# Two feed-forward up products with x as the still operand, 512 weight columns moving, and the gated block turned on TensorE

## The chip, the cores and the metric

One NeuronCore of one Trainium2 chip runs the whole program. The metric is the device time of one execution in microseconds (us). Everything is float32 at the interface; the products run as sums of three matmuls on operands that are split into a high and a low part, so one mathematical matmul is three on TensorE (PE).

## The reference, cut to what matters

Two transformer-like blocks follow one another on 256 tokens (T) by 2048 channels (D). They hold three feed-forward layers with 5632 hidden channels. The first one has a convolution over the tokens between its up product and its gate; the second and the third, which are what is changed here, do not:

```
def _swiglu(x, wg, wu, wd):
    return (jax.nn.silu(x @ wg) * (x @ wu)) @ wd

h = x
f1 = _swiglu(_rmsnorm(h, ffn1_pre_g[l]), ffn1_w_gate[l], ffn1_w_up[l], ffn1_w_down[l])
h = h + 0.5 * _rmsnorm(f1, ffn1_post_g[l])
...
f2 = _swiglu(_rmsnorm(h, ffn2_pre_g[l]), ffn2_w_gate[l], ffn2_w_up[l], ffn2_w_down[l])
h = h + 0.5 * _rmsnorm(f2, ffn2_post_g[l])
```

`wg` and `wu` are 2048 x 5632, `wd` is 5632 x 2048. The norm's factor of a token (one over the root of its mean square, called rs below) is a number per token, and so it can be multiplied in behind the product.

## The kernel before

**Units.** All large weights stream through four slots of `stage`, 1 MB each (128 partitions x 2048 float32 columns). One slot's content is a *unit*. SyncE (SP) issues one DMA per unit as soon as the unit four places ahead has been split. ScalarE (ACT, line 792) writes the high part of the slot into one of two `w_hi` buffers, VectorE (DVE, line 1303) writes the rest into `w_lo`, and PE multiplies. Semaphore `split_made` tells PE that a unit is split, `split_used` tells ACT that PE is done with the unit two before, so that its buffer can be written again. A unit is 12288 moving columns on PE wherever it is used in a feed-forward layer.

**One feed-forward layer** (`ffn(n)`, n is 0, 1 or 2; n = 1 and 2 are "the second and third") has two parts of 24 and 20 chunks of 128 hidden channels (`PARTS`). A part has an up stage, two units per chunk (88 per layer, 176 in the second and third together), and a down stage, one unit per chunk.

- *Up, before* (`wide_steps`, lines 2264 to 2268): the unit is all 2048 rows of 128 columns of gate or up. For each of its 16 row chunks the weights stand still and x moves: a matmul with `w_hi` still and 512 columns moving (the high and the low part of x side by side, line 2267), then one with `w_lo` still and 256 columns moving (line 2268). The last row chunk has the two in the other order (2264, 2265). That is 32 matmuls per unit. The results have hidden channels on the partitions and tokens along the row. Units alternate gate, up, gate, up; two of them are a *pair*. ACT copies half of a pair's sums out of PSUM (line 877), DVE adds the other half (1499), multiplies by rs (1509, from `rsb`, rs laid along the row by a small matmul in `rs_rows`, line 2422), ACT applies silu (892), DVE multiplies gate by up (1532), ACT writes `hid_hi` (897) and DVE `hid_lo` (1314). These stand between the splits in a fixed order (`up_body_order`, line 665). Most pairs run in hardware loops (`Fori`).
- *Down* (`rows_half`, line 2304): the chunk of `hid_hi` or `hid_lo` stands still and 512 weight columns move, 24 matmuls per unit (2335, 2336, 2339; in the last unit of a layer 2322 to 2324, which reports its two column quarters one after the other). The products with x itself as the still operand (`in_rows`, `out1`, `out2`) use the same lines with `xt`.

**Entering a layer.** x is turned on PE (`norm(n)`, line 2384, 128x128 transposes in groups of four: two row chunks of two token tiles), scaled into `xt` by ACT (857) and DVE (1354). `norm_done` counts the groups that are ready, eight in all. Before the third layer all 32 transposes stand ahead of the first up matmul, and for the second layer groups 0 to 3 are turned early, in the down stage ahead (`turn_early`), and groups 4 to 7 between pieces of the first two units. Those first two units are run side by side (`first_two`, `tile_part`), each piece waiting for its groups. Units 2 and 3 follow.

**Between the units of the second layer** PE also builds tables for a position bias (`bias_rows`, line 2431), after three pairs of units per side; POOL loads its inputs when DVE has written `x_nat` (`x_made`) and copies its results out, paced by `split_used`.

The engines' programs are written out by hand; each engine works in the order of its own code.

Of the kernel before, what the change touches and what calls it, by code (L numbers as in the profile page):

```python
# [24 lines left out]
F32 = mybir.dt.float32  # L25
# [13 lines left out]
PARTS = ((0, 24), (24, 20))  # L39
EPS = 1e-6  # L40
# [59 lines left out]
def build(nc, I, out):  # L100
# [10 lines left out]
    def sb(name, cols, dt=F32, at=None, parts=P):  # L111
# [32 lines left out]
    rsb = sb("rsb", T, at=TT + 6144)  # L144
# [124 lines left out]
        quarter diag_made rsb_made small_in pos_made pos_copied raw_made hn_gelu ht_made ht_copied kv_made  # L269
# [65 lines left out]
    def _(sp):  # L335
# [49 lines left out]

        def load_ffn(n):
            f = ffn_w[n]
            for part, (f0, chunks) in enumerate(PARTS):
                load(f"up{n}{part}", 4, chunks // 2, pairs(f["up"], f["off"], f0))
# [265 lines left out]
    def turn_bank(n, g):  # L655

        if n == 2:
            return (0, 1, 2, 3, 2, 3, 4, 6)[g]
        return 4 + g % 4 if n else g

    PAIR_BANK = (0, 4)

# [119 lines left out]
    def _(act):  # L782
# [35 lines left out]
        def square_pieces(e, src, p, first=0, step=2):  # L818

            for m in range(MT):  # L820
                act.wait_ge(S["piece_made"], PIECE_AT[e] + step * p + m + 1 + first // 3)
                square(src[:, span(p, m)], first + 3 * m + p, SSQ_AT[e] + step * p + m + first // 3)
# [38 lines left out]
        def ffn(n, boundary, after):  # L861
            conv = ffn_w[n]["conv"]
            for part, (f0, chunks) in enumerate(PARTS):
# [6 lines left out]
                def e0(j, s):  # L870

                    act.wait_ge(split_used, 2 * j + (before + 4))
                    if conv:
                        act.wait_ge(S["pair_d1"], j + (q0 + 1))
                    else:
                        act.wait_ge(S["pair_d2"], j + (q0 - 1))
# [12 lines left out]
                def e2(j, s):  # L889
                    act.wait_ge(S["pair_d1"], j + (q0 + 3))  # L890
                    src = conv_a[:, s * T:(s + 1) * T] if conv else turn[:, s * 512:s * 512 + T]
                    act.activation(conv_a[:, s * T:(s + 1) * T], src, ACT.Silu).then_inc(S["pair_e2"], 1)
# [7 lines left out]
                up_phase(act, lambda i, u: split(name, 4, i, u), e2, e3, e1 if conv else nothing, chunks, split_down,  # L900
                         boundary=None if part else boundary, s0=e0)
                for u in range(2, chunks):
                    split_down(u)
                    if part:
# [138 lines left out]
        def enter_ffn1(split):  # L1043

            split(0)
            split(1)
            square_pieces(2, x_nat, 1, 0, 4)
            scaled_hi(2, 4, C_F1)
            scaled_hi(2, 5, C_F1)
            square_pieces(2, f_nat, 1, 6, 4)  # L1050
            square_pieces(2, x_nat, 2, 0, 4)
            scaled_hi(2, 6, C_F1)
            scaled_hi(2, 7, C_F1)
            square_pieces(2, f_nat, 2, 6, 4)
            root(2, 4)
# [15 lines left out]
        def enter_ffn2(split):  # L1071
# [4 lines left out]
            for g in range(4):  # L1076
                scaled_hi(4, g, C_F2)
            act.wait_ge(S["piece_made"], NEW_AT[6] + 4)
            for m in range(MT):
                square(x_nat[:, m * D:m * D + HALF], 2 * m, SSQ_AT[7] + m)  # L1080
            for g in range(4, 8):
# [1941 lines left out]
```

## Time and profile before

| | |
|---|---|
| median of 3 runs | 3593.45 us (3589.94 to 3593.74) |
| the profiled execution | 3594.03 us, span 3592.1 us |
| PE matmul busy | 3425.2 us, 95% |
| DVE busy | 2130.7 us, 59% |
| ACT busy | 1636.2 us, 46% |
| DMA | mean 198 GB/s |

The span runs from the first to the last instruction, and 1.9 us of the execution lie around it. Matmul durations in the rows run from a matmul's start to its modelled end, and matmuls overlap; the pace of PE is read from start to start.

### The profile page before, as it was taken

Reading aid. Unit: us, or ns where it says so; the run is one execution under the profiler, and the core shown is the slowest. Engines: PE = TensorE matmul, PEld = TensorE weight load, DVE = VectorE, ACT = ScalarE, POOL = GpSimd, SP = SyncE. Lnnn points to the kernel's source line nnn. Section 1 sums busy time; section 2 is a strip of 40 time slices with the busy share of each in tenths; the row PEclk is TensorE's granted clock in tenths of the full one; section 3 lists DMA queues with packets and bytes.
Section 4 is the critical chain, followed back from the end, with each engine's and each line's share of the span. In section 5 each row is a group of like instructions: output and inputs, shape, how many; then the busy total and the mean of one; then the engine's idle time right before and its main releaser. Section 6 shows DMA issues by size and latency. Waiting matters only on the chain.

```text
span 3592.1 us, 49777 instructions
## 1 busy us (share of the span) xinstructions
PE 3425.2 (95%) x19694; PEld 2919.4 (81%) x19694; DVE 2130.7 (59%) x2280; ACT 1636.2 (46%) x1772; POOL 346.2 (10%) x411
## 2 busy tenths in 40 slices
PE   5899889999999999999999899999999899999998
PEld 1786678888888888888888799898888788888886
DVE  0774657775566565544555578895455555545555
ACT  0333346653455455543443455663443555434443
POOL 1110000000000000000000147661000000000000
PEclk7899999999999999999999999999899999999999
DMA  9998657776666667976665656667235566666664
GB/s 398 297 340 299 221 167 225 225 227 221 188 187 195 189 186 164 204 206 189 187 187 188 175 149 156 168 179 232 91 106 187 153 187 186 187 189 188 185 188 139
DMA packets 813373, 712.54 MB, mean 198 GB/s; under 512 B 13127, under 2 KB 742527, under 8 KB 805696
## 3 DMA queue, kind: packets, MB, share of 16 engines
q1 hardware_dynamic: 787840, 627.09, 58.9%
q0 software_dynamic: 20624, 79.44, 7.8%
q10 hardware_dynamic: 4784, 4.27, 0.4%
q8 instruction: 88, 1.44, 0.2%
q14 instruction: 37, 0.30, 0.0%
HBM read 698.94 MB, written 11.80 MB: 198 GB/s over the span
## 4 chain that ended last, share of the span: by engine, by line
PE 78%; DVE 9%; ACT 4%; DMA 4%; issue 3%; POOL 1%; ACTq 0%; DVEq 0%; SPq 0%; POOLq 0%
PE ps L2267 24%; PE ps L2268 12%; PE ps L2335 8%; PE ps L2336 8%; PE ps L2339 8%; DVE w_lo L1303 3%; ACT w_hi L792 3%; DMA stage<-in_w_ada 2%; PE ps L2286 2%; PE ps L2287 2%; PE ps L2288 2%; PE ps L2265 2%; PE ps L2299 1%; PE ps L2495 1%; PE ps L2300 1%
## 5 line engine op out<-in xcount | busy, mean ns | idle before, releaser
L1303 DVE TENSOR_TENSOR w_lo<-stage,w_hi 128x2048 fp32r<-128x2048 f32 x528 | 1221.4, 2313 | 1093.7 <-ACT w_hi L792 1092.6
L792 ACT ACTIVATE w_hi<-stage 128x2048 fp32r<-128x2048 f32 x528 | 1010.8, 1914 | 1483.5 <-PE ps L2265 617.0
L2267 PE MATMUL ps<-xt,w_hi 128*128 128x512 f32 x3960 | 1416.2, 400 | 11.3 <-DVE w_lo L1303 10.1
L2268 PE MATMUL ps<-xt,w_lo 128*128 128x256 f32 x3960 | 1114.1, 281 | 0.0
L2267 PEld LDWEIGHTS ps<-xt,w_hi 128*128 128x128 f32 x3960 | 746.9, 189 | 187.8 <-DVE w_lo L1303 14.5
L2268 PEld LDWEIGHTS ps<-xt,w_lo 128*128 128x128 f32 x3960 | 750.9, 190 | 11.8
L2335 PE MATMUL ps<-w_hi,hid_hi 128*128 128x512 f32 x1152 | 449.2, 390 | 5.8 <-DVE w_lo L1303 5.8
L2336 PE MATMUL ps<-w_lo,hid_hi 128*128 128x512 f32 x1152 | 448.2, 389 | 0.0
L2286 PE MATMUL ps<-xt,w_hi 128*128 128x256 f32 x1184 | 342.2, 289 | 18.9 <-DVE w_lo L1303 16.6
L2339 PE MATMUL ps<-w_hi,hid_lo 128*128 128x512 f32 x1152 | 354.7, 389 | 0.0
L2287 PE MATMUL ps<-xt,w_hi 128*128 128x256 f32 x1184 | 337.0, 285 | 0.0
L2288 PE MATMUL ps<-xt,w_lo 128*128 128x256 f32 x1184 | 336.8, 284 | 0.0
L2335 PEld LDWEIGHTS ps<-w_hi,hid_hi 128*128 128x128 f32 x1152 | 216.2, 188 | 52.4 <-DVE w_lo L1303 4.3
L2286 PEld LDWEIGHTS ps<-xt,w_hi 128*128 128x128 f32 x1184 | 229.0, 193 | 29.8 <-issue 23.6
L2339 PEld LDWEIGHTS ps<-w_hi,hid_lo 128*128 128x128 f32 x1152 | 216.2, 188 | 45.0
L2336 PEld LDWEIGHTS ps<-w_lo,hid_hi 128*128 128x128 f32 x1152 | 216.3, 188 | 44.7
L2287 PEld LDWEIGHTS ps<-xt,w_hi 128*128 128x128 f32 x1184 | 229.3, 194 | 0.0
L2288 PEld LDWEIGHTS ps<-xt,w_lo 128*128 128x128 f32 x1184 | 229.1, 193 | 0.0
L2335 PE MATMUL ps<-w_hi,xt 128*128 128x512 f32 x248 | 98.4, 397 | 8.7 <-issue 3.2
L2265 PE MATMUL ps<-xt,w_hi 128*128 128x512 f32 x264 | 105.4, 399 | 0.0
L2495 PE MATMUL ps<-stage,csilu 128*32 128x512 f32 x384 | 68.3, 808 | 33.6 <-DMA stage<-in_w_ada 33.1
L2336 PE MATMUL ps<-w_lo,xt 128*128 128x512 f32 x248 | 97.2, 392 | 0.0
(414 smaller groups left out, 3649.9 us busy)
## 6 DMA issues: line engine op xcount, KB each, us to landing
stage<-in_w_in SPq DMA_DIRECT2D x92, 1024.0 KB, 5.7
stage<-in_w_up SPq DMA_DIRECT2D x88, 1024.0 KB, 5.8
stage<-in_ffn_w_gate SPq DMA_DIRECT2D x88, 1024.0 KB, 5.6
stage<-in_ffn_w_up SPq DMA_DIRECT2D x88, 1024.0 KB, 5.6
stage<-in_ffn_w_down SPq DMA_DIRECT2D x88, 1024.0 KB, 5.5
stage<-in_w_ada SPq DMA_DIRECT2D x48, 1024.0 KB, 8.8
stage<-in_w_down SPq DMA_DIRECT2D x44, 1024.0 KB, 5.1
late<-in_w_ada POOLq DMA_DIRECT2D x64, 512.0 KB, 6.7
```

The source lines that it names most:

```text
L792: act.activation(w_hi[:, u % 2 * UNIT:(u % 2 + 1) * UNIT], slot(u % SLOTS), ACT.Copy).then_inc(hi_made, 1)
L1303: dve.tensor_tensor(w_lo[:, part], slot(u % SLOTS), w_hi[:, part].bitcast(F32), ALU.subtract).then_inc(split_made, 1)
L2265: last = pe.matmul(dst, wh, both(k), start=False, stop=True)
L2267: pe.matmul(dst, wh, both(k), start=k == 0, stop=False)
L2268: last = pe.matmul(dst[:, T:2 * T], wl, chunk(xt_hi, k), start=False, stop=False)
L2286: pe.matmul(dst, wh, chunk(xh, k0 + k), start=start and k == 0, stop=False)
L2287: pe.matmul(dst, wh, chunk(xl, k0 + k), start=False, stop=False)
L2288: last = pe.matmul(dst, wl, chunk(xh, k0 + k), start=False, stop=stop and k == n - 1)
L2335: pe.matmul(rows_cols(half, m, n, 512, swapped), a, wh, start=st, stop=False)
L2336: pe.matmul(rows_cols(half, m, n, 512, swapped), a, wl, start=False, stop=False)
L2339: last = pe.matmul(rows_cols(half, m, n, 512, swapped), b, wh, start=False, stop=en)
L2495: last = pe.matmul(ps[32 * j:32 * j + 32, b * 512:(b + 1) * 512], weight.to_broadcast([P, 32]), part[:, j % 2 * 512:(j % 2 + 1) * 512], st ...
```

## The change

In the second and third layer (`ffn_rows(n)` on ACT, DVE and PE takes the place of `ffn(n)`), the hidden channels go by *blocks* of four chunks: six blocks in the first part, five in the second, 22 in the two layers.

- A unit of the up stage is now 512 rows (four row chunks) of 512 weight columns of gate or up. A block has 8 units: gate and up by turns for each of four groups of rows. SP loads it so (`blocks_of`), with runs of 512 columns per row where there were 128.
- On PE a row chunk of x for one token tile stands still and 512 weight columns move: x high by `w_hi`, x high by `w_lo`, x low by `w_hi`, 24 matmuls per unit. The sums of a block stand in four banks with tokens on the partitions (gate: two, up: two), blocks alternate between the two halves of PSUM.
- rs is now a number per partition: ACT reads the gate's bank, scales by rs and applies silu in one instruction (`gate`, two per block), DVE multiplies up's bank by rs and by that (`product`, two per block, into `h_blk`). PE turns `h_blk` by eight 128x128 transposes (`turn_hid`) after the second unit of the next block, back into the gate's two banks; ACT and DVE make `hid_hi` and `hid_lo` from there (`hidden`, two instructions each). `rs_rows`, `take_rs` and `rsb` are gone.
- No hardware loop is left in these two layers.
- The entry: only groups 0 and 1 of x must be ready for units 0 and 1, two more groups for each further pair of units. The transposes of the rest stand behind unit 0, 1 (and 2 for the third layer), four row chunks each. ACT's and DVE's splits, squares and scalings are put in a matching order.
- `bias_rows` stands behind unit 11, as before behind 12 units, and uses other banks. Which half of the down product takes which banks is exchanged between the parts.

The core of the diff:

```diff
+        def blocks_of(ws, f0):
+            views = [w.rearrange("(c k p) n -> c p k n", p=P, k=4) for w in ws]
+            return lambda i, u: [(slot(u % SLOTS).rearrange("p (k n) -> p k n", k=4),
+                                  views[u % 2][u // 2][:, :, ds(i * 512 + f0 * P, 512)])]
...
+                def unit(v):
+                    j, u = divmod(v, 8)
+                    pe.wait_ge(split_made, plan[up][1] + v + 1)
+                    for kk in range(4):
+                        k, at = 4 * (u // 2) + kk, v % 2 * UNIT + kk * 512
+                        wh, wl = (w[:, at:at + 512] for w in (w_hi, w_lo))
+                        for m in range(MT):
+                            dst = bank(block_bank(j, u % 2, m))
+                            pe.matmul(dst, chunk(xt_hi, k, m), wh, start=k == 0, stop=False)
+                            pe.matmul(dst, chunk(xt_hi, k, m), wl, start=False, stop=False)
+                            last = pe.matmul(dst, chunk(xt_lo, k, m), wh, start=False, stop=k == KC - 1)
+                    last.then_inc(split_used, 1)
...
+                def turn_hid(j):
+                    pe.wait_ge(S["pair_d2"], block_at(n, part, j) + 1)
+                    for c in range(4):
+                        for m in range(MT):
+                            last = pe.transpose(bank(block_bank(j, 0, c // 2), c % 2 * T + m * P, P),
+                                                h_blk[:, m * 512 + c * P:m * 512 + (c + 1) * P], ident[:, :])
+                    last.then_inc(S["hid_turned"], 1)
...
+                    unit(v)
+                    if part == 0 and j == 0:
+                        between(u)
+                    if j and u == 1:
+                        turn_hid(j - 1)
+                    if n == 1 and part == 0 and v == 11:
+                        bias_rows()
...
-        norm(4)
-        ffn(2)
+        norm(4, range(2))
+        def norm_ffn2(u):
+            if u < 3:
+                norm(4, range(2 + 2 * u, 4 + 2 * u))
+        ffn_rows(2, norm_ffn2)
```

ACT and DVE, per block j (v counts the units of the part, u those of the block; DVE's `product` stands at u == 1, all `hidden` at u == 3):

```diff
+                def gate(j):
+                    act.wait_ge(S["norm_rs"], ROOT_AT[RS_ROOT[n]] + 1)
+                    act.wait_ge(split_used, plan[up][1] + 8 * j + 9)
+                    for m in range(MT):
+                        at = RS_COL[n] + m
+                        last = act.activation(turn[:, m * 512:(m + 1) * 512], bank(block_bank(j, 0, m)), ACT.Silu,
+                                              scale=stats[:, at:at + 1])
+                    last.then_inc(S["pair_e2"], 1)
...
+                def product(j):
+                    dve.wait_ge(S["pair_e2"], block_at(n, part, j) + 1)
+                    dve.wait_ge(split_used, plan[up][1] + 8 * j + 10)
+                    for m in range(MT):
+                        last = dve.scalar_tensor_tensor(out=h_blk[:, m * 512:(m + 1) * 512],
+                                                        in0=bank(block_bank(j, 1, m)), scalar=stats[:, at:at + 1],
+                                                        in1=turn[:, m * 512:(m + 1) * 512], op0=ALU.mult, op1=ALU.mult)
+                    last.then_inc(S["pair_d2"], 1)
```

**Where the order moves, first place.** PE at the entry of the third layer, behind the last down matmuls of the product ahead (`out2`; `ident` marks a transpose). Before:

```order
L2323 MATMUL ps<-w_lo,hid_hi 128x512
L2324 MATMUL ps<-w_hi,hid_lo 128x512
L2384 MATMUL ps<-ident,x_nat 128x128 x32
L2267 MATMUL ps<-xt,w_hi 128x512
L2268 MATMUL ps<-xt,w_lo 128x256
```

And now:

```order
L2432 MATMUL ps<-w_hi,hid_lo 128x512
L2492 MATMUL ps<-ident,x_nat 128x128 x8
L2585 MATMUL ps<-w_hi,xt 128x512
L2586 MATMUL ps<-w_lo,xt 128x512
L2587 MATMUL ps<-w_hi,xt 128x512
...
L2492 MATMUL ps<-ident,x_nat 128x128 x8
L2585 MATMUL ps<-w_hi,xt 128x512
```

Eight transposes are ahead of the first up matmul instead of 32; the other 24 stand in eights behind units 0, 1 and 2.

**Second place.** DVE at the same entry (L1445 and L1509 write the new x, L1354 and L1423 its scaled low part, L1303 and L1372 split a unit). Before:

```order
L1445 SCALAR_TENSOR_TENSOR x_nat<-f_nat,stats,x_nat 128x512 x4
L1354 SCALAR_TENSOR_TENSOR xt<-ps,cols,xt 128x256 x4
L1303 TENSOR_TENSOR w_lo<-stage,w_hi 128x2048
L1445 SCALAR_TENSOR_TENSOR x_nat<-f_nat,stats,x_nat 128x512 x2
L1354 SCALAR_TENSOR_TENSOR xt<-ps,cols,xt 128x256 x4
L1445 SCALAR_TENSOR_TENSOR x_nat<-f_nat,stats,x_nat 128x512 x2
L1354 SCALAR_TENSOR_TENSOR xt<-ps,cols,xt 128x256 x8
L1319 TENSOR_REDUCE stats<-stats 128x2
L1323 TENSOR_SCALAR stats<-stats 128x2
L1303 TENSOR_TENSOR w_lo<-stage,w_hi 128x2048
```

And now:

```order
L1509 SCALAR_TENSOR_TENSOR x_nat<-f_nat,stats,x_nat 128x512 x2
L1423 SCALAR_TENSOR_TENSOR xt<-ps,cols,xt 128x256 x4
L1372 TENSOR_TENSOR w_lo<-stage,w_hi 128x2048
L1509 SCALAR_TENSOR_TENSOR x_nat<-f_nat,stats,x_nat 128x512 x4
L1423 SCALAR_TENSOR_TENSOR xt<-ps,cols,xt 128x256 x4
L1372 TENSOR_TENSOR w_lo<-stage,w_hi 128x2048
L1509 SCALAR_TENSOR_TENSOR x_nat<-f_nat,stats,x_nat 128x512 x2
L1423 SCALAR_TENSOR_TENSOR xt<-ps,cols,xt 128x256 x4
L1372 TENSOR_TENSOR w_lo<-stage,w_hi 128x2048
L1423 SCALAR_TENSOR_TENSOR xt<-ps,cols,xt 128x256 x4
L1372 TENSOR_TENSOR w_lo<-stage,w_hi 128x2048 x2
```

The splits of units 1, 2 and 3 now stand behind two groups of x each, where the split of unit 2 stood behind all eight; the sums for rs come behind the split of unit 5.

**Third place.** DVE in the steady up stage, one block (L1635 is `product`, L1646 `hidden`):

```order
L1372 TENSOR_TENSOR w_lo<-stage,w_hi 128x2048 x6
L1635 SCALAR_TENSOR_TENSOR h_blk<-ps,stats,turn 128x512 x2
L1372 TENSOR_TENSOR w_lo<-stage,w_hi 128x2048 x2
L1646 TENSOR_TENSOR hid_lo<-ps,hid_hi 128x512 x2
L1372 TENSOR_TENSOR w_lo<-stage,w_hi 128x2048 x6
```

Four instructions beside eight splits stand where 16 stood (1499, 1509, 1532 and 1314 for each of four pairs).

## Rows read from the trace of the kernel before

**Rows 1.** Cores: span and mean granted TensorE clock.

```profile
core 0: 3592.1 us, clock 0.970
```

**Rows 2.** Page, part 1: busy us (share), instructions.

```profile
PE 3425.2 (95%) x19694; PEld 2919.4 (81%) x19694; DVE 2130.7 (59%) x2280; ACT 1636.2 (46%) x1772; POOL 346.2 (10%) x411
```

**Rows 3.** Page, part 4: chain that ended last, by engine.

```profile
PE 78%; DVE 9%; ACT 4%; DMA 4%; issue 3%; POOL 1%; ACTq 0%; DVEq 0%; SPq 0%; POOLq 0%
```

**Rows 4.** Page, part 5, costliest group of PE: busy us, mean ns, idle before.

```profile
L2267 PE MATMUL ps<-xt,w_hi 128*128 128x512 f32 x3960 | 1416.2, 400 | 11.3 <-DVE w_lo L1303 10.1
```

**Rows 5.** Timeline, ACT, second layer's up stage: start us, us, form [idle before <-releaser].

```profile
1689.93 1.92 ACT L792 ACTIVATE w_hi<-stage 128x2048 fp32r<-128x2048 f32 x1 [3.73 <-PE ps L2265]
...
1708.65 0.58 ACT L877 ACTIVATE turn<-ps 128x512 f32<-128x512 f32 x1
...
1785.97 1.92 ACT L792 ACTIVATE w_hi<-stage 128x2048 fp32r<-128x2048 f32 x1 [3.44 <-PE ps L2265]
```

**Rows 6.** Timeline, ACT, the product out2 (x-shaped operand still).

```profile
2763.94 1.92 ACT L792 ACTIVATE w_hi<-stage 128x2048 fp32r<-128x2048 f32 x1 [3.52 <-PE ps L2339]
...
2785.70 1.92 ACT L792 ACTIVATE w_hi<-stage 128x2048 fp32r<-128x2048 f32 x1 [3.52 <-PE ps L2339]
```

**Rows 7.** Timeline, PE, last down unit of the first layer and the matmul behind it.

```profile
1254.69 0.39 PE L2322 MATMUL ps<-w_hi,hid_hi 128*128 128x512 f32 x1
...
1260.13 0.39 PE L2267 MATMUL ps<-xt,w_hi 128*128 128x512 f32 x1
```

**Rows 8.** Timeline, PE and ACT, around the early transposes of the first layer's down stage.

```profile
1242.84 0.60 PE L2384 MATMUL ps<-ident,f_nat 128*128 128x128 f32 x4
...
1243.10 1.91 ACT L792 ACTIVATE w_hi<-stage 128x2048 fp32r<-128x2048 f32 x1 [2.88 <-PE ps L2339]
...
1249.02 1.92 ACT L792 ACTIVATE w_hi<-stage 128x2048 fp32r<-128x2048 f32 x1 [3.27 <-PE ps L2339]
```

**Rows 9.** Windows: us, then PE, PEld, DVE, ACT, POOL busy, PEclk, DMA share, GB/s.

```profile
1233.00:1255.00 22.00, 22.00 (x104) 18.17 (x104) 12.41 (x12) 12.44 (x19) 0.00 (x0) 1.00 0.60 173
1260.00:1303.00 43.00, 38.56 (x218) 32.27 (x217) 31.26 (x42) 25.48 (x39) 7.61 (x13) 1.00 0.70 192
2824.00:2837.00 13.00, 7.00 (x33) 6.42 (x34) 11.97 (x21) 7.75 (x18) 0.00 (x0) 0.63 0.53 163
2837.00:2851.00 14.00, 13.19 (x65) 11.16 (x64) 3.62 (x7) 6.05 (x10) 0.00 (x0) 0.85 0.00 1
```

**Rows 10.** Timeline, DVE, entry of the third layer.

```profile
2826.88 1.66 DVE L1354 SCALAR_TENSOR_TENSOR xt<-ps,cols,xt 128x256 fp32r<-128x256 f32 x4 [0.70 <-ACT xt L857]
2828.46 2.28 DVE L1303 TENSOR_TENSOR w_lo<-stage,w_hi 128x2048 fp32r<-128x2048 f32 x1
2830.66 1.41 DVE L1445 SCALAR_TENSOR_TENSOR x_nat<-f_nat,stats,x_nat 128x512 f32<-128x512 f32 x2
...
2854.44 0.68 DVE L1499 TENSOR_TENSOR turn<-turn,ps 128x512 f32<-128x512 f32 x1
```

**Rows 11.** Timeline, PE, entry of the third layer.

```profile
2824.79 3.29 PE L2384 MATMUL ps<-ident,x_nat 128*128 128x128 f32 x16 [6.55 <-DVE x_nat L1445]
...
2836.82 0.78 PE L2267 MATMUL ps<-xt,w_hi 128*128 128x512 f32 x1
...
2851.78 0.50 PE L2267 MATMUL ps<-xt,w_hi 128*128 128x512 f32 x1 [1.60 <-DVE w_lo L1303]
```

**Rows 12.** Timeline, ACT, entry of the third layer: splits of units 2, 5 and 6.

```profile
2847.49 1.92 ACT L792 ACTIVATE w_hi<-stage 128x2048 fp32r<-128x2048 f32 x1 [6.60 <-PE ps L2265]
...
2863.72 1.92 ACT L792 ACTIVATE w_hi<-stage 128x2048 fp32r<-128x2048 f32 x1 [2.33 <-PE ps L2265]
...
2869.28 1.92 ACT L792 ACTIVATE w_hi<-stage 128x2048 fp32r<-128x2048 f32 x1 [2.85 <-PE ps L2265]
```

**Rows 13.** Timeline, PE and ACT, entry of the second layer.

```profile
1278.32 0.50 PE L2267 MATMUL ps<-xt,w_hi 128*128 128x512 f32 x1 [1.79 <-DVE w_lo L1303]
...
1296.62 1.92 ACT L792 ACTIVATE w_hi<-stage 128x2048 fp32r<-128x2048 f32 x1 [3.65 <-PE ps L2265]
```

More of the change, by code:

```diff
@@ L39 @@
 PARTS = ((0, 24), (24, 20))
+BLOCKS = tuple(chunks // 4 for _, chunks in PARTS)
 EPS = 1e-6
@@ L903, in ffn, with ffn_rows, hidden @@
                     split_down(u)
+                    if part:
+                        after(u)
+        def ffn_rows(n, enter, after):
+            for part, (f0, chunks) in enumerate(PARTS):
+                up, down = f"up{n}{part}", f"down{n}{part}"
+                def gate(j):
[6 more added lines that the diff above has]
+                    last.then_inc(S["pair_e2"], 1)
+                def hidden(j):
+                    act.wait_ge(S["hid_turned"], block_at(n, part, j) - FC + 1)
+                    for b in range(2):
+                        at = (4 * j + 2 * b) * T
+                        act.activation(hid_hi[:, at:at + 512], bank(block_bank(j, 0, b)), ACT.Copy).then_inc(S["pair_e3"], 1)
+                for v in range(8 * BLOCKS[part]):
+                    if part or v > 4:
+                        split(up, 0, 0, v)
+                    elif v == 0:
+                        enter(lambda u: split(up, 0, 0, u))
+                    j, u = divmod(v, 8)
+                    if part == 0 and v == 5:
+                        root(RS_ROOT[n], 4 if n == 1 else 2)
+                    if j and u == 0:
+                        gate(j - 1)
+                    elif j and u == 3:
+                        hidden(j - 1)
+                for u in range(chunks):
+                    split(down, 0, 0, u)
+                    if u == 0:
+                        gate(BLOCKS[part] - 1)
+                    elif u == 3:
+                        hidden(BLOCKS[part] - 1)
                     if part:
@@ L1286, in _ @@
                 keep_root_table()
-        ffn(2, enter_ffn2, after_post(8))
+        ffn_rows(2, enter_ffn2, after_post(8))
         post_root(8)
@@ L1363, in spread_rs @@
             last.then_inc(S["diag_made"], 1)
-        def take_rs(count):
-            dve.wait_ge(S["rsb_made"], count)
-            link.then(dve.tensor_copy(rsb[:, :], bank(7, 0, T)))
         def quarter_done(e, p, name):
@@ L1489, in ffn @@
                 pb = PAIR_BANK[part]
-                gating = n == 0 and part == 0
+                gating = part == 0
                 def split_down(u):
@@ L2471, in ffn @@
                     first_pairs()
-                if n == 1 and part == 0:
-                    pairs(1, 3)
-                    bias_rows()
-                    pairs(3, chunks // 2)
-                else:
-                    pairs(part == 0, chunks // 2)
-                if n == 0 and part:
+                pairs(part == 0, chunks // 2)
+                if part:
                     pe.wait_ge(S["mod_made"], 6)
                 rows_phase(f"down{n}{part}", chunks // 2, hid_hi, hid_lo, part == 0, q0 + 2, last=part == 1,
-                           after=turn_early if n == 0 and part else nothing)
+                           after=turn_early if part else nothing)
```

309 lines of the change are left out of this document (183 added, 126 removed).

## The prediction

> **What bounds the kernel now.** I read the cores view first: one core, granted clock 0.970 [rows 1], so PE runs at full clock nearly everywhere. Then the page: PE is busy 95% of the span, DVE 59%, ACT 46% [rows 2], and 78% of the chain that ended last is PE's own work [rows 3]. The largest group is the wider of the up product's two matmul forms [rows 4]; its idle time before is 11.3 us over all layers, so PE is not waiting there, it is working. What matters is therefore PE's pace per unit, and a matmul's printed duration doesn't give it, since matmuls overlap. I take it from ACT: it splits unit v+2 at the moment at which PE is done with unit v (its idle time ends "<-PE"), so the distance of its splits is PE's time for one unit.
>
> - Up, before: 17 splits from 1689.93 to 1785.97 [rows 5] are 96.04 / 17 = 5.65 us a unit.
> - Still operand x-shaped, 512 weight columns moving: four splits from 2763.94 to 2785.70 [rows 6] are 5.44 us a unit.
> - The very order of three that the change uses (one bank, high by high, high by low, low by high): 24 matmuls from 1254.69 to the next unit's 1260.13 [rows 7] are again 5.44 us, 227 ns each.
>
> All three have 12288 moving columns, 5.12 us at 2.4 GHz. The rest is a price per matmul: 0.32 / 24 = 13 ns in the new form, 0.53 / 32 = 17 ns in the old.
>
> **The change, part by part.**
>
> *Pace of the up stage.* 176 units, 8 matmuls fewer in each: 176 x (5.65 - 5.44) = **37 us less**, all of it on the path, since PE sets it. The bounds: 0 if the 5.65 us belong to the up stage and not to the form, and 37 us. I take 37, because [rows 7] is the same form down to the order. Here the Trainium skill speaks against the change ("TensorE: Matmul & The Clock Gate", the section on why the gap is 56 ns and not 53.3): a fixed cost of about 2.5 ns per matmul. By that eight matmuls fewer would save 0.02 us a unit, 3.5 us in all, and the change would lose. The trace disagrees, with 13 ns over the column time in a stream where each matmul has its own weight load.
>
> *Turning the gated block.* 22 blocks x 8 transposes stand in PE's stream, and nothing hides them. Four transposes in a down stage stretch a unit from 5.44 to 1249.02 - 1243.10 = 5.92 us [rows 8]: 0.12 us each. Eight of them are 0.95 us, and 22 x 0.95 = **21 us more**. From above: at the cold pace, 16 in 3.29 us [rows 11], it would be 1.65 us a block, 36 us. From below 0.8 us a block, 18 us, if the switch to and from transposes costs once and not twice. I take 0.95, since the clock was 1.00 around such transposes [rows 9] (first line).
>
> *Does PE wait for them?* `turn_hid` waits for `product`. Call the start of a block's first unit 0. The last up unit before it ended at 0; then ACT splits (1.92 us), DVE splits (2.29), and DVE's two products run to about 4.3 + 2 x 0.7 = 5.8 us [rows 5, 10]. PE asks at 2 x 5.44 = 10.9 us. Slack 5 us, no wait. `hidden` comes behind the split of unit 3: ACT needs 1.92 + 2 x 0.58, DVE 4.3 + 2 x 0.68, both under the 5.44 us until their next turn plus the time ACT has in front; no split is late. Its gate's banks are used again only a block later. The work that ACT and DVE lose (each has four instructions beside the splits of a block, where DVE had 16 and ACT 12) was hidden behind PE, and gives nothing.
>
> *Loads.* SP issues as many units as before, 1 MB each, in 2 KB runs where there were 512 B. The DMA share around the entry is 0.70 [rows 9] (second line) and the prefetch is three units deep; at 5.44 us a unit 193 GB/s are needed, which the down stages already draw. Nothing for the path. POOL's table copies are paced by PE's units and only move with them; its inputs for `bias_rows` wait for `x_made`, now after unit 8, with more than 20 us until PE asks after unit 11. `bias_rows` itself costs what it cost.
>
> *Entry of the third layer.* Before: the first up matmul at 2836.82 [rows 11], although x was ready for the first four row chunks at 2826.88 + 1.66 = 2828.5 [rows 10]; unit 2 waited 1.60 us for its split [rows 11]; unit 4 was done when the split of unit 6 began, 2869.28 [rows 12]. Now unit 0 starts at 2828.6. It runs partly at a low clock, as before (0.85 over the 14 us from 2837 [rows 9] (fourth line): 13.2 us busy for two units of 5.65, 1.9 us lost): done at 2828.6 + 5.44 + 1.9 = 2835.9. Each of units 1, 2 and 3 needs eight transposes (0.95) and 5.44: 2855.1. In that time ACT must wait for PE's transposes, scale two groups (1.8 us) and split, then DVE splits: about 6.2 us behind the transposes, which just fits for units 2 and 3; for unit 4 it ends 0.7 us late. Unit 4 done at 2861.2, 8.1 us earlier. Five units of 0.21 are counted above, so the entry itself gives **7 us**.
>
> *Entry of the second layer.* Before: the two first units run in pieces between transposes, unit 2 waits 1.79 us for its split, and unit 4 is done at 1296.62 [rows 13]. Now unit 0 runs whole from 1260.13 to 1265.6. ACT's squares, now ahead of its splits, delay the split of unit 1 to 1267.0 and of unit 2 to 1275.0, two PE gaps of 0.4 and 1.5 us; units 3 and 4 follow without one, and unit 4 ends at 1291.4. That is 5.2 us earlier, less 1.0 counted above: **4 us**. Both entries are worked out from chains of five or six instructions, and I hold either as good to 3 us.
>
> *Sum*: -37 + 21 - 7 - 4 = -27. The profiled execution took 3594.03 us, 0.6 above the median of the three runs: 3594.0 - 27 = **3567 us**.
>
> **The rivals.**
>
> *A. The entries give nothing*, because ACT, which now stands still for PE's transposes with a split behind it, is late at each of them. For it: each engine works in its written order, and my margins at units 2 and 3 are below 0.5 us. Against: the old entry of the third layer had PE idle or cold for 8 us, and something of it must come back. -37 + 21 = -16: 3578 us.
>
> *B. No gain of pace; slower than before.* The 5.65 us are not the form's, but come from what goes on beside an up stage (PSUM reads by ACT and DVE while PE accumulates). For it: an up unit ahead of the loop took 2869.28 - 2863.72 = 5.56 us [rows 12], so something but the form moves the pace by 0.1. Against: [rows 7], the same form at 5.44. Then 3594 + 21 - 11 = 3604 us. It decides when a unit takes more than about 5.6 us.
>
> *C. The clock falls at the turns.* Transposes replace dense work 22 times; [rows 9] (third and fourth line) show 0.63 in a stretch of transposes with idle time between them and 0.85 after it, 1.9 us lost. At every block it is 22 x 1.9 = 42 us: 3567 + 42 = 3609 us, also slower. Against: with four transposes in each of four units the clock stayed at 1.00 [rows 9] (first line), and with two sets of eight between short gaps too [rows 9] (second line). The Trainium skill ("TensorE: Matmul & The Clock Gate", Part 4) says that transposes don't count as PE-busy; the trace shows no fall around eight of them.
>
> *D. The turns cost their upper bound* (36 us) and the entries half: -37 + 36 - 5 = -6, 3588 us, about no change.
>
> **How the numbers follow.** The forecast with its bounds (turns 18 to 24, entries 11 +- 4): 0.68. A or a part of it: 0.18. D: 0.04. B: 0.05, C: 0.03. A gain larger than 36 us, from something I don't see: 0.02. About 0.2%, 7 us, can be told from no change. Faster by more than that holds the forecast, A and the last: 0.89; the same: 0.04; slower: 0.07 with the rare cases that nobody thought of. The range takes in the forecast's bounds and A, from 3556 to 3582; B, C and D are left out.
>
> **What would show it.** In the changed profile: ACT's splits in the second and third up stages 5.44 us apart, 6.4 once a block; about 1230 fewer matmuls on PE (176 x 8, less 176 transposes); granted clock 1.00 in the steady stages; the first up matmul of the third layer 3.8 us after its first transpose, and not 2836.82 - 2824.79 = 12.0 us [rows 11]. I would be wrong if the splits stood 5.6 us apart (B), if the clock row showed dips with the period of a block (C), or if PE's idle time ended on DVE's `w_lo` at every entry unit (A).

## The result, and the profile after

The changed kernel takes 3562.45 us (median of 4 runs, 3560.88 to 3566.2), the kernel before 3593.59 us (4 runs): a ratio of 0.9917, with a 95% interval of 0.9901 to 0.9933, which is 24 to 36 us less. The forecast was 3567 us, in a range of 3556 to 3582, and faster with a chance of 0.89. Spans of unchanged code differ from run to run by up to 10 us (experiment 6), so what the change is worth is read stage by stage below.

| | before | after |
|---|---|---|
| profiled span | 3592.1 us | 3559.6 us |
| PE busy, matmuls recorded | 3425.2 us, 19694 | 3403.8 us, 18458 |
| DVE busy | 2130.7 us | 2017.6 us |
| ACT busy | 1636.2 us | 1528.3 us |

The page of the changed kernel: busy times, the chain that ended last, and one of the three new groups of matmuls:

```profile
PE 3403.8 (96%) x18458; PEld 2863.0 (80%) x18458; DVE 2017.6 (57%) x2010; ACT 1528.3 (43%) x1554; POOL 346.1 (10%) x411
...
PE 79%; DVE 9%; ACT 4%; DMA 4%; issue 3%; POOL 1%; ACTq 0%; SPq 0%; DVEq 0%; POOLq 0%
...
L2585 PE MATMUL ps<-w_hi,xt 128*128 128x512 f32 x1408 | 552.3, 392 | 3.4 <-DVE xt L1423 1.8
```

PE has 1236 matmuls fewer, and is still what bounds the kernel: these lines answer to [rows 2 to 4]. ACT and DVE are some 110 us less busy each, and nothing of that shows in the time.

ACT's splits in the second layer's up stage, one block of the changed kernel (columns: start us, duration us, form, idle before and its releaser):

```profile
1688.33 1.92 ACT L812 ACTIVATE w_hi<-stage 128x2048 fp32r<-128x2048 f32 x1 [3.52 <-PE ps L2587]
...
1710.09 1.92 ACT L812 ACTIVATE w_hi<-stage 128x2048 fp32r<-128x2048 f32 x1 [3.52 <-PE ps L2587]
1711.92 1.25 ACT L934 ACTIVATE turn<-ps,stats 128x512 f32<-128x512 f32 x2
...
1726.42 1.91 ACT L812 ACTIVATE w_hi<-stage 128x2048 fp32r<-128x2048 f32 x1 [3.53 <-PE ps L2587]
1728.23 1.07 ACT L943 ACTIVATE hid_hi<-ps 128x512 fp32r<-128x512 f32 x2
1732.77 1.92 ACT L812 ACTIVATE w_hi<-stage 128x2048 fp32r<-128x2048 f32 x1 [3.47 <-PE ps L2587]
```

Four splits in 21.76 us are 5.44 us a unit, against 5.65 in [rows 5]; the interval with the turn, 1726.42 to 1732.77, is 6.35 us. The idle time before a split ends on PE each time: PE sets the pace and neither ACT nor DVE is late. The window over that stretch (us, then PE, PEld, DVE, ACT, POOL busy, PEclk, DMA share, GB/s) has the granted clock at 1.00, as in the steady stage of the kernel before:

```profile
1700.00:1800.00 100.00, 100.00 (x451) 82.95 (x450) 46.29 (x26) 38.98 (x27) 0.00 (x0) 1.00 0.59 190
```

**Where the time went, layer by layer.** For the second layer take the first up matmul, 1260.13 [rows 7], and the second split behind the layer; for the third the first and the last split of the layer.

Before, ACT:

```profile
2022.83 1.91 ACT L792 ACTIVATE w_hi<-stage 128x2048 fp32r<-128x2048 f32 x1
...
2812.90 1.92 ACT L792 ACTIVATE w_hi<-stage 128x2048 fp32r<-128x2048 f32 x1 [3.52 <-PE ps L2339]
...
3567.05 1.92 ACT L792 ACTIVATE w_hi<-stage 128x2048 fp32r<-128x2048 f32 x1 [3.52 <-PE ps L2339]
```

After, PE and ACT:

```profile
1256.54 0.39 PE L2585 MATMUL ps<-w_hi,xt 128*128 128x512 f32 x1
...
2006.36 1.89 ACT L812 ACTIVATE w_hi<-stage 128x2048 fp32r<-128x2048 f32 x1
...
2795.41 1.92 ACT L812 ACTIVATE w_hi<-stage 128x2048 fp32r<-128x2048 f32 x1 [3.52 <-PE ps L2447]
...
3534.56 1.92 ACT L812 ACTIVATE w_hi<-stage 128x2048 fp32r<-128x2048 f32 x1 [3.52 <-PE ps L2447]
```

Second layer: 762.7 us before, 749.8 after, 12.9 less. Third: 754.2 and 739.1, 15.0 less. Together 27.9 us, where 27 were forecast. The span fell by 32.5 us. The other 4.6 us lie in stretches with unchanged code; experiment 6 asks whether they belong to the change or to the run.

### The profile page after: what moved, and what is told of

It reads as the page before. It is cut to its first block, busy times and chain, and to the rows that moved or that the text cites. A ratio compares the mean times of both kernels' runs of the same rounds, so it can differ in the third digit from the quotient of the medians.

```text
span 3559.6 us, 45278 instructions
## 1 busy us (share of the span) xinstructions
PE 3403.8 (96%) x18458; PEld 2863.0 (80%) x18458; DVE 2017.6 (57%) x2010; ACT 1528.3 (43%) x1554; POOL 346.1 (10%) x411
## 3 DMA queue, kind: packets, MB, share of 16 engines
q8 instruction: 120, 1.97, 0.2%
## 4 chain that ended last, share of the span: by engine, by line
PE 79%; DVE 9%; ACT 4%; DMA 4%; issue 3%; POOL 1%; ACTq 0%; SPq 0%; DVEq 0%; POOLq 0%
PE ps L2585 9%; PE ps L2587 9%; PE ps L2586 9%; PE ps L2443 9%; PE ps L2444 8%; PE ps L2447 8%; PE ps L2375 7%; PE ps L2376 3%; DVE w_lo L1372 3%; ACT w_hi L812 3%; DMA stage<-in_w_ada 3%; PE ps L2394 2%; PE ps L2396 2%; PE ps L2395 2%; PE ps L2407 1%
## 5 line engine op out<-in xcount | busy, mean ns | idle before, releaser
L1372 DVE TENSOR_TENSOR w_lo<-stage,w_hi 128x2048 fp32r<-128x2048 f32 x528 | 1221.4, 2313 | 1176.0 <-ACT w_hi L812 1175.2
L2585 PE MATMUL ps<-w_hi,xt 128*128 128x512 f32 x1408 | 552.3, 392 | 3.4 <-DVE xt L1423 1.8
L2586 PE MATMUL ps<-w_lo,xt 128*128 128x512 f32 x1408 | 549.6, 390 | 0.0
L2587 PE MATMUL ps<-w_hi,xt 128*128 128x512 f32 x1408 | 549.6, 390 | 0.0
L2375 PE MATMUL ps<-xt,w_hi 128*128 128x512 f32 x1320 | 472.3, 400 | 6.2 <-DVE w_lo L1372 6.2
L2376 PE MATMUL ps<-xt,w_lo 128*128 128x256 f32 x1320 | 371.3, 281 | 0.0
L2396 PE MATMUL ps<-xt,w_lo 128*128 128x256 f32 x1184 | 337.4, 285 | 0.0
L2585 PEld LDWEIGHTS ps<-w_hi,xt 128*128 128x128 f32 x1408 | 265.4, 188 | 59.1 <-issue 2.3
L2587 PEld LDWEIGHTS ps<-w_hi,xt 128*128 128x128 f32 x1408 | 265.4, 188 | 55.6
L2586 PEld LDWEIGHTS ps<-w_lo,xt 128*128 128x128 f32 x1408 | 265.5, 189 | 54.7
L2375 PEld LDWEIGHTS ps<-xt,w_hi 128*128 128x128 f32 x1320 | 248.7, 188 | 66.9 <-DVE w_lo L1372 9.7
L2394 PEld LDWEIGHTS ps<-xt,w_hi 128*128 128x128 f32 x1184 | 229.5, 194 | 29.9 <-issue 23.6
L2376 PEld LDWEIGHTS ps<-xt,w_lo 128*128 128x128 f32 x1320 | 250.1, 189 | 3.6
```

What stands on the lines that cost most here:

```text
L1372: dve.tensor_tensor(w_lo[:, part], slot(u % SLOTS), w_hi[:, part].bitcast(F32), ALU.subtract).then_inc(split_made, 1)
L2375: pe.matmul(dst, wh, both(k), start=k == 0, stop=False)
L2376: last = pe.matmul(dst[:, T:2 * T], wl, chunk(xt_hi, k), start=False, stop=False)
L2394: pe.matmul(dst, wh, chunk(xh, k0 + k), start=start and k == 0, stop=False)
L2585: pe.matmul(dst, chunk(xt_hi, k, m), wh, start=k == 0, stop=False)
L2586: pe.matmul(dst, chunk(xt_hi, k, m), wl, start=False, stop=False)
```

## The experiments

**1. Equal lengths side by side, in the old form.** The largest term of the prediction was the pace. Is it the new layout that makes a unit cheaper? The kernel before, every second row chunk with its two matmuls exchanged (`e1_hllh`):

```diff
-                if k == KC - 1:
+                if k % 2:
                     pe.matmul(dst[:, T:2 * T], wl, chunk(xt_hi, k), start=False, stop=False)
-                    last = pe.matmul(dst, wh, both(k), start=False, stop=True)
+                    last = pe.matmul(dst, wh, both(k), start=False, stop=k == KC - 1)
```

> The kernel before, with one edit: in the old up form every second row chunk takes its two matmuls in the other order, so that equal lengths stand side by side (512, 256, 256, 512, 512 ...). Still 32 matmuls and 12288 columns a unit, nothing else moves. Theory 1 (a fixed price of 13 ns per matmul, and 3 to 4 ns more wherever the length changes from one matmul to the next): half the changes of length go, so a unit falls from 5.65 to 5.55 to 5.60 us, and over 264 units the kernel is 13 to 26 us faster. Theory 2 (the up stage's 5.65 us come from what ACT and DVE do beside it): the unit stays at 5.65 us, no change of the time. Theory 3 (the price is only a matter of the number of matmuls): also 5.65 us.

Measured: 3573.51 us against 3598.7, ratio 0.993 (0.9913 to 0.9947); the second number is the kernel before, run along with it, here and below. ACT's splits, the first and the 18th of a stretch of its trace:

```profile
1700.29 1.92 ACT L792 ACTIVATE w_hi<-stage 128x2048 fp32r<-128x2048 f32 x1 [3.35 <-PE ps L2265]
...
1795.03 1.92 ACT L792 ACTIVATE w_hi<-stage 128x2048 fp32r<-128x2048 f32 x1 [2.87 <-PE ps L2265]
```

94.74 / 17 = 5.573 us a unit. The second layer is 8.1 us shorter than before, the third 6.6, the first 3.7. (1.6 of the 8.1 lie in the interval with `bias_rows`, 18.08 us and not 19.71; see the last section.) So of the 0.21 us a unit that the change won, 0.08 came free by an exchange of neighbours with the same 32 matmuls, the same loads and no turning. Theories 2 and 3 fall. Set beside the turns, the new layout's pace is 5.44 + 0.92 / 8 = 5.555 us a unit, only 0.018 us better than the reordered old form, about 3 us over 176 units. The rest of what the layout is worth beyond that order lies in the entries. The hardware loops that the change removes are no rival for the pace: in the trace of before, PE's first matmul of a steady unit starts 236 ns behind the last one of the unit ahead, no more than inside a unit.

Start to start in that trace:

```profile
1711.93 0.40 PE L2267 MATMUL ps<-xt,w_hi 128*128 128x512 f32 x1
1712.17 0.28 PE L2268 MATMUL ps<-xt,w_lo 128*128 128x256 f32 x1
1712.28 0.27 PE L2264 MATMUL ps<-xt,w_lo 128*128 128x256 f32 x1
1712.39 0.40 PE L2265 MATMUL ps<-xt,w_hi 128*128 128x512 f32 x1
1712.63 0.39 PE L2267 MATMUL ps<-xt,w_hi 128*128 128x512 f32 x1
```

From the first to the last of these, with one of each kind of neighbours, 0.70 us pass; 1536 columns at 2.4 GHz are 0.64 us.

**2. The same in fours** (`e7_fours`): the old form with four of 512, eight of 256, eight of 512 and so on.

```diff
+            if len(ks) == KC:
+                for g in range(4):
+                    for wide in ((True, False) if g % 2 == 0 else (False, True)):
+                        for k in range(4 * g, 4 * g + 4):
+                            w = (w_hi if wide else w_lo)[:, at + k * P:at + (k + 1) * P]
+                            if wide:
+                                last = pe.matmul(dst, w, both(k), start=k == 0, stop=k == KC - 1)
+                            else:
+                                last = pe.matmul(dst[:, T:2 * T], w, chunk(xt_hi, k), start=False, stop=False)
+                return last
```

> The kernel before with the old up form's matmuls in fours of equal length (four of 512, eight of 256, eight of 512 ...): 4 changes of length per unit where there were 31 and 16 in the first reordering. Theory 1 (13.3 ns per matmul, and more only at a change of length): the unit falls from 5.57 us to 5.12 + 32 x 13.3 ns = 5.55 us or a little less (5.53 if the price goes on falling in a line with the changes). Rival (what helped in the first reordering was not equal neighbours but the alternation of still operands): back towards 5.65 us.

Measured: one run, 3585.22 us.

```profile
1701.13 1.92 ACT L792 ACTIVATE w_hi<-stage 128x2048 fp32r<-128x2048 f32 x1 [3.37 <-PE ps L2267]
...
1751.41 1.92 ACT L792 ACTIVATE w_hi<-stage 128x2048 fp32r<-128x2048 f32 x1 [2.88 <-PE ps L2267]
```

50.28 / 9 = 5.587 us: neither 5.55 nor 5.65, and no better than pairs. Both expectations miss. In the middle of a run of equal lengths the distances are 227 ns for 512 columns and 120 for 256, just 13.3 ns over the columns. That holds with weights standing still as here and with x standing still as in the changed kernel, so which operand stands still doesn't matter. The first ones behind a change of length differ: the first distance behind the change to 256 columns is 113 ns, 7 less than in the middle, and the first five behind the change to 512 columns are 234, 236, 228, 232 and 231 ns, together 26 more. That the price has a part per matmul and a part that hangs on the neighbours is shown; what makes the second part is open.

**3. The turns, twice and a quarter.** The changed kernel with each transpose issued twice (`e2_turn_twice`), and with only the last chunk's two of the eight (`e3_turn_quarter`):

```diff
                         for m in range(MT):
-                            last = pe.transpose(bank(block_bank(j, 0, c // 2), c % 2 * T + m * P, P),
-                                                h_blk[:, m * 512 + c * P:m * 512 + (c + 1) * P], ident[:, :])
+                            for _ in range(2):
+                                last = pe.transpose(bank(block_bank(j, 0, c // 2), c % 2 * T + m * P, P),
+                                                    h_blk[:, m * 512 + c * P:m * 512 + (c + 1) * P], ident[:, :])
```

```diff
                         for m in range(MT):
-                            last = pe.transpose(bank(block_bank(j, 0, c // 2), c % 2 * T + m * P, P),
-                                                h_blk[:, m * 512 + c * P:m * 512 + (c + 1) * P], ident[:, :])
+                            if c == 3:
+                                last = pe.transpose(bank(block_bank(j, 0, c // 2), c % 2 * T + m * P, P),
+                                                    h_blk[:, m * 512 + c * P:m * 512 + (c + 1) * P], ident[:, :])
```

> The changed kernel with each of the eight transposes of a block issued twice (16 per block, same result). Theory 1 (the turns lie on the path at 0.12 us each, at full clock): the long split interval once a block goes from 6.36 to 7.25 to 7.3 us, granted clock stays 1.00 in the steady stages, span 19 to 21 us longer. Rival (transposes let the clock fall, the change was just below that point): the clock in the up windows falls below 1.00, units after a turn take longer than 5.44 us, span over 40 us longer.

> The changed kernel with only two of the eight transposes of a block, those of the last chunk; the hidden values of the other three chunks are then not the gated ones, so that part of the computation is left out. Theory 1: the long interval falls from 6.36 to about 5.70 us (0.109 us less for each transpose left out, 0.16 stay for going to transposes and back), span 14 us shorter. Rival (a turn's cost is mostly the change to transposes and back, or a wait for DVE's product): it stays above 6.1 us, span less than 6 us shorter.

Measured, one run each: 3583.59 and 3553.29 us. The interval with the turn, with 16 transposes:

```profile
1733.32 1.92 ACT L812 ACTIVATE w_hi<-stage 128x2048 fp32r<-128x2048 f32 x1 [3.53 <-PE ps L2587]
...
1740.55 1.92 ACT L812 ACTIVATE w_hi<-stage 128x2048 fp32r<-128x2048 f32 x1 [4.35 <-PE ps L2587]
```

7.23 us, and with two:

```profile
1727.83 1.92 ACT L812 ACTIVATE w_hi<-stage 128x2048 fp32r<-128x2048 f32 x1 [3.52 <-PE ps L2587]
...
1733.54 1.92 ACT L812 ACTIVATE w_hi<-stage 128x2048 fp32r<-128x2048 f32 x1 [2.82 <-PE ps L2587]
```

5.71 us. Over a unit of 5.44 this is 0.27 us for 2 transposes, 0.91 for 8 and 1.79 for 16: 0.109 us for each, and 0.05 for going there and back (the expectation had 0.16 for that, which doesn't fit its own 5.70 us). The two layers are 16.0 us longer with twice the transposes, not 19 to 21: 3.2 of that are missing at `bias_rows`, whose long interval was 16.40 us in that run and 19.63 in the changed kernel, where the granted clock stood at 0.50 for 6.8 us and 13.7 us (last section). With a quarter they are 14.3 us shorter, as expected. A window of the run with 16 transposes (columns as above):

```profile
1710.00:1810.00 100.00, 100.00 (x459) 83.26 (x458) 44.80 (x27) 39.20 (x28) 0.00 (x0) 1.00 0.58 186
```

The clock stays at 1.00, that is 2.4 GHz, at twice the turning, in the third layer too. Rival C falls, and with room to spare.

**4. Unit 0 of the third layer later** (`e4_entry_four`):

```diff
-        norm(4, range(2))
+        norm(4, range(4))
         def norm_ffn2(u):
-            if u < 3:
+            if 1 <= u < 3:
                 norm(4, range(2 + 2 * u, 4 + 2 * u))
```

> The changed kernel; at the entry of the third layer PE turns groups 0 to 3 of x ahead of unit 0 instead of groups 0 and 1. Theory 1 (the entry gains because unit 0 starts with a quarter of x, and each unit covers the next groups): unit 0 starts when DVE has written the next piece of x, about 5 us later (8.9 us behind the first transpose instead of 3.8), one set of eight transposes is saved later, and unit 4 is done 4 us later than in the changed kernel. Rival (the start of unit 0 doesn't matter, since ACT and DVE set the pace of units 1 to 4 anyway): unit 4 is done at the same time, within 1 us.

One run, 3573.58 us. The changed kernel's entry, PE and ACT (the splits of units 5 and 6; that of unit 6 begins when unit 4 is done):

```profile
2807.30 1.97 PE L2492 MATMUL ps<-ident,x_nat 128*128 128x128 f32 x8 [6.55 <-DVE x_nat L1509]
2811.11 0.79 PE L2585 MATMUL ps<-w_hi,xt 128*128 128x512 f32 x1 [1.84 <-DVE xt L1423]
...
2838.78 1.92 ACT L812 ACTIVATE w_hi<-stage 128x2048 fp32r<-128x2048 f32 x1 [0.36 <-PE ps L2587]
2844.51 1.92 ACT L812 ACTIVATE w_hi<-stage 128x2048 fp32r<-128x2048 f32 x1 [0.97 <-PE ps L2587]
```

With four groups first (2832.45 is unit 1's first matmul):

```profile
2817.29 1.97 PE L2492 MATMUL ps<-ident,x_nat 128*128 128x128 f32 x8 [6.55 <-DVE x_nat L1509]
2824.63 1.97 PE L2492 MATMUL ps<-ident,x_nat 128*128 128x128 f32 x8 [5.37 <-DVE x_nat L1509]
2826.25 0.78 PE L2585 MATMUL ps<-w_hi,xt 128*128 128x512 f32 x1
...
2832.45 0.39 PE L2585 MATMUL ps<-w_hi,xt 128*128 128x512 f32 x1
...
2856.57 1.92 ACT L812 ACTIVATE w_hi<-stage 128x2048 fp32r<-128x2048 f32 x1 [0.96 <-PE ps L2587]
```

Unit 0 starts 8.96 us behind the first transpose, as expected, and 5.15 us later than in the changed kernel. But unit 4 is done only 2.1 us later (39.3 us behind the first transpose and not 37.2), between the two expectations, which both miss. 0.9 us of the difference is the set of transposes that is saved later. The other 2.2 us are unit 0's own: from its first matmul it takes 6.2 us here, and 8.4 in the changed kernel. PE that starts sooner spent more of its first unit at the low clock here. The windows show it, the first of the changed kernel, the second of `e4_entry_four`:

```profile
2811.10:2817.10 6.00, 5.99 (x14) 4.74 (x15) 4.89 (x5) 0.00 (x0) 0.00 (x0) 0.50 0.44 137
...
2826.20:2827.60 1.40, 1.40 (x5) 1.19 (x4) 0.88 (x3) 1.26 (x4) 0.00 (x0) 0.50 0.99 386
```

0.50 is 1.2 GHz. The changed kernel's unit 0 runs at it for 6.0 us, the other one's for 1.4; behind that the clock is 1.00.

**5. Both entries mended** (`e5_entries`): ACT's splits ahead of its squares in the second layer, and matmuls without use in PE's idle time ahead of the third.

```diff
             split(0)
-            square_pieces(2, x_nat, 1, 0, 4, 4)
             split(1)
-            square_pieces(2, x_nat, 2, 0, 4, 6)
+            square_pieces(2, x_nat, 1, 0, 4, 4)
             split(2)
+            square_pieces(2, x_nat, 2, 0, 4, 6)
...
+        def warm(count):
+            for _ in range(count):
+                pe.matmul(bank(0), hid_hi[:, 0:P], hid_hi[:, 0:512], start=True, stop=True)
+        pe.wait_ge(S["rows_taken"], 2 * rows_index["out2"] + 2)
+        warm(12)
         norm(4, range(2))
+        warm(8)
```

> The changed kernel with two edits at the entries. Second layer: ACT's splits of units 1 and 2 go back ahead of its squares. Third layer: 12 matmuls without use ahead of the first transposes and 8 behind them, into a bank that unit 0 overwrites, as soon as DVE has read the product ahead. Theory 1 (the entries still lose 0.6 and 1.3 us to late splits and 2.9 us to a low clock in unit 0, the latter because PE was idle ahead): the two gaps of the second layer close, unit 4 done about 1.8 us earlier; in the third layer unit 0 takes 5.5 to 6 us instead of 8.4, unit 4 done 2.5 to 3.5 us earlier, 34 us behind the first transpose instead of 37.2; together 4 to 5 us, 0.13% of the time. Rival (ACT and DVE set the pace of units 2 to 4 there): unit 0 is shorter, but unit 3 or 4 waits for its split and unit 4 is done less than 1 us earlier.

Measured: 3558.69 us against 3595.9, ratio 0.9895 (0.988 to 0.991). In the second layer, from the first up matmul (of the changed kernel: 1256.54, above) to the end of unit 4, when ACT splits unit 6, it is 31.31 us in the changed kernel and 29.27 here:

```profile
1287.86 1.92 ACT L812 ACTIVATE w_hi<-stage 128x2048 fp32r<-128x2048 f32 x1 [0.28 <-PE ps L2587]
```

```profile
1259.82 0.39 PE L2585 MATMUL ps<-w_hi,xt 128*128 128x512 f32 x1
...
1289.10 1.92 ACT L812 ACTIVATE w_hi<-stage 128x2048 fp32r<-128x2048 f32 x1 [0.28 <-PE ps L2587]
```

In the third, PE's first groups (L3098 are the matmuls without use):

```profile
2807.11 1.97 PE L2492 MATMUL ps<-ident,x_nat 128*128 128x128 f32 x8 [1.96 <-DVE x_nat L1509]
2808.73 2.90 PE L3098 MATMUL ps<-hid_hi 128*128 128x512 f32 x8
2811.48 0.40 PE L2585 MATMUL ps<-w_hi,xt 128*128 128x512 f32 x1
```

its window over unit 0 (columns as above):

```profile
2811.00:2816.80 5.80, 5.80 (x27) 4.79 (x26) 4.80 (x5) 0.00 (x0) 0.00 (x0) 1.00 0.44 138
```

and the split of unit 6:

```profile
2841.91 1.92 ACT L812 ACTIVATE w_hi<-stage 128x2048 fp32r<-128x2048 f32 x1 [0.94 <-PE ps L2587]
```

The clock is 1.00 in unit 0, and unit 4 is done 34.8 us behind the first transpose and not 37.2. The second layer gained 2.0 us (about 1.8 expected), the third 2.4, just short of the 2.5 to 3.5 expected. Unit 0 itself is 2.9 us shorter, 5.5 us as expected, but it starts 4.4 us behind the first transpose and not 3.8: the eight matmuls without use, 2.9 us long and begun at the low clock, still ran when x was ready. The low clock in unit 0 was the price of the idle time ahead of it, since filling that time takes it away. A further 1.6 us came at `bias_rows`, where nothing was edited.

**6. The changed kernel once more** (`after_again`), unedited.

> The changed kernel once more, unedited, on the same chip as the others of this call: a ratio to the kernel before within 0.990 to 0.993, and the same splits: 5.44 us a unit, 6.36 once a block. The stretches that the change doesn't touch should differ from run to run by some us and show whether the 4.6 us of the span's gain outside the two layers belong to the change (then they come back) or to the run (then they don't).

Measured: 3567.09 us against 3595.9, ratio 0.9915 (0.9901 to 0.9928). The two layers took 749.8 and 739.1 us, the same as in the first profile to 0.1 us. All else took 2077.6 us of the span, 2070.7 in the first profile of the changed kernel and 2075.3 in that of before; over the seven profiles in which none of that was edited it went from 2070.7 to 2080.7. The 4.6 us outside the two layers did not come back, and lie within that spread, so they belong to the run. The change is worth the 27.9 us; this second comparison of medians gives 28.8.

**7. All together** (`e6_all`): experiment 5, and the order of experiment 1 where the old form is left, which is the first layer above all.

> The changed kernel with both edits at the entries (as in the run before) and, in the first layer and wherever else the old up form is left, the order 512, 256, 256, 512 of the first experiment. Theory: the terms add up, since all of them are PE time on the path: the two layers 28 us and 6 us less than before as measured, the first layer 4 us less as in the first experiment (766 instead of 770 us), together 38 us, a ratio of 0.989 to 0.990 and a median near 3556 us. Rival (the first layer's up stage is bound by DVE's late sums there, so that PE's pace is lost again): the first layer stays at 770 us, ratio 0.990 to 0.991.

Measured: 3550.02 us against 3594.29, ratio 0.9883 (0.9866 to 0.9899). The first layer took 766.0 us (before 769.7, from ACT's second split of the layer to its second split of the next), the two others 746.2 and 735.9: 38.5 us over all three, 38 expected. The rival falls. The medians are 44 us apart and the ratio is below the 0.989 expected; the other 6 us lie in unedited code, which took 2069.4 us here, a little less than the least in experiment 6. The first transposes of the third layer, with the same edit as in experiment 5:

```profile
2798.66 1.09 PE L2492 MATMUL ps<-ident,x_nat 128*128 128x128 f32 x8 [1.96 <-DVE x_nat L1509]
2799.51 2.09 PE L3098 MATMUL ps<-hid_hi 128*128 128x512 f32 x8
2802.01 0.50 PE L2585 MATMUL ps<-w_hi,xt 128*128 128x512 f32 x1 [0.41 <-DVE xt L1423]
...
2832.60 1.92 ACT L812 ACTIVATE w_hi<-stage 128x2048 fp32r<-128x2048 f32 x1 [0.94 <-PE ps L2587]
```

Here the clock was 1.00 already at the transposes (1.09 us for eight, 1.97 in experiment 5), unit 0 starts 3.4 us behind the first of them, and unit 4 is done at 33.9 us, the 34 that experiment 5 had expected. This is the fastest kernel of the study, and its interval lies below that of the changed kernel.

## Why the prediction was right

*The pace*, forecast 176 x 0.21 = 37 us: a unit takes 5.44 us, as [rows 7] had it, in every steady unit of both layers. The weighing of the row against the 2.5 ns per matmul of the Trainium skill ("TensorE: Matmul & The Clock Gate", the section on why the gap is 56 ns and not 53.3) came out for the row: with 24 matmuls of 512 columns a unit is 0.32 us over its columns. The step had a hole all the same. I had two candidate reasons, the number of matmuls and something of the up stage, and took all of 0.21 for the first. Eight matmuls fewer at the 13.3 ns of experiment 2 are 0.106 us, half of it. The other half comes from unequal lengths side by side, and experiment 1 takes 0.076 of it back by an exchange of order, without a new layout. The sum was right because rows 5 to 7 measured both forms whole; the reason given for it was right by half.

*The turns*, forecast 0.95 us a block: measured 0.91 to 0.92, with 0.109 for a transpose; 20 us and not 21. They lay wholly on the path, as said: the interval follows the number of transposes at 2, 8 and 16. Nothing waited for `product` or `hidden`: ACT's idle time before every steady split ends on PE.

*The entries.* The second layer: unit 4 done 5.2 us sooner forecast; from the first up matmul it was 36.49 us before and 31.31 after, 5.2. The two gaps of PE, forecast 0.4 and 1.5 us, were 0.43 and 1.09. The third layer, unit 4 done: 8.1 us forecast, 7.3 found (44.5 us behind the first transpose before, 37.2 after). Here a term was mis-sized: I priced unit 0's low clock as before, at 1.9 us, but it was 2.9. The low clock ended 6.0 us behind the first up matmul in the changed kernel (window above), and 4.4 us in the kernel before:

```profile
2836.80:2841.20 4.40, 4.40 (x15) 3.76 (x14) 2.14 (x7) 3.62 (x9) 0.00 (x0) 0.50 0.00 0
```

Why it lasted longer is open. It is not that the 24 further transposes raise the clock before unit 0: in `e1_hllh`, whose entry is the old one, it stayed at 0.50 over all of them, and the low clock still ended 4.4 us behind the first up matmul, at 2829.25:

```profile
2817.00:2829.20 12.20, 7.16 (x32) 6.42 (x33) 11.28 (x20) 7.63 (x18) 0.00 (x0) 0.50 0.52 173
2829.20:2833.60 4.40, 4.40 (x15) 3.79 (x14) 2.17 (x7) 3.65 (x9) 0.00 (x0) 0.50 0.00 0
```

A second term was mis-sized the other way: unit 4's split, forecast 0.7 us late, held PE up by 0.15 us (its first matmul starts 381 ns behind unit 3's last, where 227 is the pace). The start itself was forecast 3.8 us behind the first transpose and was 3.8. Less the pace of their units, counted above, the entries gave 4.1 and 6.2 us, 10 and not 11.

*What was costed at nothing* stayed so: loads, POOL's copies, the removed work of ACT and DVE, and `bias_rows` (19.71 us before, 19.63 after). That the load's longer runs matter nowhere was not tried by itself; the idle times before the splits show no wait for a load in the steady stages.

*Rivals.* A didn't happen, though ACT was late twice: the splits of units 1 and 2 of the second layer cost 2 us, which experiment 5 took back, and the third layer had next to none. B fell to the 5.44 us of every steady unit, with ACT and DVE reading PSUM beside them; what moves the pace besides the number of matmuls is the order of lengths. C fell to experiment 3, D to the interval of 6.35 us. The chances given to the forecast, A and the last case add up to 0.88, not 0.89.

*The total* was 3567 forecast, 3562.45 and, repeated, 3567.09 measured. Against the stretches the terms are -37, +20, -10, together -27, and 27.9 us were found in the two layers; that the second median falls on the forecast to 0.1 us is luck, with a spread of 10 us in the unedited code.

## What to carry to other kernels

Read PE's pace from start to start, or from the engine that waits for it, and divide what is over columns / clock by the number of matmuls: here it was 13 ns each, so fewer and longer matmuls pay, but a form that needs transposes behind it gives most of that back (1.68 us won in a block, 0.92 paid, and 0.6 of the 1.68 was to be had by order alone). Before changing a layout, try the order: strict alternation of unequal matmuls cost 0.08 us a unit here, and an exchange of two lines took it back. A layout in which work can begin with a quarter of its input pays at a serial entry: the two entries gave 10 us, the steady state 17, of which 14 were to be had by the order. What PE loses there to the low clock can be bought back with matmuls into an unused bank while it would idle (2.4 us in experiment 5 and 3.3 in experiment 7), as long as they end before the input is ready.

## What the runs showed of the hardware

- A matmul of 512 columns in a steady stream of its like starts 227 ns after the one before, one of 256 columns 120 ns: 13.3 ns over the columns at 2.4 GHz in both. The same still operand twice in a row (x high with `w_hi`, then with `w_lo`; it is loaded again each time, 18458 loads for 18458 matmuls) made no difference: each of the three distances of the changed kernel is 226 or 227 ns.
- Where lengths alternate, the price depends on the neighbours: 5.65 us a unit for strict alternation, 5.573 in pairs, 5.587 in fours, each with 32 matmuls.
- A 128x128 float32 transpose in a dense stream costs 0.109 us, a group of them 0.05 us more, and the granted clock stayed at 1.00 with 16 in a row once in eight units (experiment 3).
- The interval with `bias_rows` and the unit behind it, from split to split, took 19.6 to 19.7 us in six of the ten profiles, 18.0 to 18.1 in three (`e1_hllh`, `e5_entries`, `e6_all`) and 16.4 in one (`e2_turn_twice`), with no edit to `bias_rows`. The difference is the clock: it was granted at 0.50 for 13.7, 10.2 and 6.8 us. The windows of the longest and the shortest, `after` and `e2_turn_twice`:

```profile
1328.90:1342.60 13.70, 13.70 (x58) 12.89 (x58) 2.86 (x2) 0.00 (x0) 0.55 (x1) 0.50 0.15 59
```

```profile
1337.90:1344.70 6.80, 6.80 (x27) 6.18 (x27) 2.76 (x2) 0.00 (x0) 0.55 (x1) 0.50 0.10 39
```

In each of the ten the clock fell while the narrow matmuls of `bias_rows` (16 moving columns each) ran. What decides when it falls and when it rises again was not looked for.
